# Two weight rings of unequal depth, the residual kept in DRAM, and gathers with an index bound, in a decoder layer with routed experts

## What is computed

```
x1     = x + gate1 * mixer(x)                       # the residual
h      = norm_modulate(x1)                          # rows of 1024 channels
scores = sigmoid(h @ w_router)                      # 64 experts in 8 groups
idx    = top 6 of the experts in the best 4 groups  # per token
routed = sum over the 6 of w * (silu(h @ w_gate[e]) * (h @ w_up[e])) @ w_down[e]
shared = (silu(h @ w_sg) * (h @ w_su)) @ w_sd
y      = norm_modulate(x1 + gate2 * (routed + shared))
```

## Time and profile before

| | us |
|---|---|
| three runs | 2287.98 (2282.24 to 2290.77), median and ends |
| profiled execution | 2288.57 |
| its span, first to last instruction | 2286.8 |
| TensorE busy | 1946.5 (85%) |
| VectorE / ScalarE / GpSimd busy | 869.4 / 470.1 / 217.9 |
| mean granted TensorE clock | 0.887 |

### The profile page before, as it was taken

One profiled execution on the slowest core, in us unless ns is written; L12 is line 12 of the kernel. 1 busy time (PEld: TensorE's weight loads), 2 busy tenths in 40 slices (PEclk: granted clock), 3 DMA queues, 4 the chain that ended last, 5 costly groups with the idle time before them and its releaser, 6 DMA issues.

```text
span 2286.8 us, 25257 instructions
## 1 busy us (share of the span) xinstructions
PE 1946.5 (85%) x8864; PEld 996.8 (44%) x8864; DVE 869.4 (38%) x2376; ACT 470.1 (21%) x899; POOL 217.9 (10%) x178
## 2 busy tenths in 40 slices
PE   3669899999988887979978989999999999895570
PEld 1146555554456663335555434444444443342230
DVE  4844711001255553222236234334433434331139
ACT  0121101210045551130143111111111111110022
POOL 0000001000000000030000011222122212111010
PEclk7679757899999999989987999999999999997785
DMA  8921002000102002521006179999999998896554
GB/s 293 358 54 51 3 0 116 1 0 1 74 13 71 1 1 92 186 102 55 0 39 155 47 291 313 350 358 348 342 354 346 368 376 280 282 330 221 202 166 179
DMA packets 98489, 389.72 MB, mean 170 GB/s; under 512 B 26879, under 2 KB 29603, under 8 KB 68780
## 3 DMA queue, kind: packets, MB, share of 16 engines
q1 hardware_dynamic: 79356, 318.89, 37.4%
q0 software_dynamic: 19008, 69.21, 11.6%
HBM read 329.43 MB, written 57.07 MB: 169 GB/s over the span
## 4 chain that ended last, share of the span: by engine, by line
PE 41%; DMA 6%; issue 5%; DVE 3%; ACT 2%; SPq 0%; POOL 0%; POOLq 0%; DVEq 0%; ACTq 0%
PE psum L1000 20%; PE psum L1011 9%; DMA arena<-in_w_exp_up 6%; PE psum L856 5%; PE psum L981 3%; PE psum L890 1%; PE psum L880 1%; PE psum L897 1%; PE psum L1018 1%; DVE arena L1686 1%; DVE arena L1675 0%; DVE arena L1687 0%; DVE arena L1676 0%; PE psum L835 0%; DVE arena L1674 0%
## 5 line engine op out<-in xcount | busy, mean ns | idle before, releaser
L1000 PE MATMUL psum<-arena 128*32 128x512 f32 (+2 forms) x2016 | 483.1, 614 | 86.1 <-DMA arena<-in_w_exp_up 84.8
L1000 PEld LDWEIGHTS psum<-arena 128*32 128x32 f32 (+2 forms) x2016 | 175.9, 143 | 340.1 <-issue 330.2
L1011 PE MATMUL psum<-arena,tail 128*32 128x512 f32 (+2 forms) x1000 | 231.6, 595 | 0.0
L1625 DVE TENSOR_TENSOR arena<-arena,psum 128x256 f32<-128x256 f32 x65 | 39.5, 608 | 445.2 <-ACT arena L1945 442.1
L2069 POOL DMA_INDIRECT moe_rows<-arena x64 | 101.6, 1588 | 682.6 <-DVE arena L1653 377.3
L1945 ACT ACTIVATE arena<-psum 128x256 f32<-128x256 f32 x65 | 24.9, 383 | 550.2 <-PE psum L1000 550.2
L704 PE MATMUL psum<-arena 128*128 128x512 f32 (+1 forms) x384 | 127.2, 495 | 0.0
L1011 PEld LDWEIGHTS psum<-arena,tail 128*32 128x32 f32 (+2 forms) x1000 | 79.9, 138 | 105.3 <-issue 105.3
L856 PE MATMUL psum<-arena 128*128 128x512 f32 (+1 forms) x288 | 124.3, 593 | 0.9 <-ACT arena L1871 0.5
L745 PE MATMUL psum<-arena 128*128 128x512 f32 (+2 forms) x192 | 85.0, 558 | 10.4 <-ACT arena L1801 10.4
L856 PEld LDWEIGHTS psum<-arena 128*128 128x128 f32 (+1 forms) x288 | 68.5, 239 | 55.3 <-issue 40.1
(11 more groups left out here) (478 smaller groups left out, 2436.6 us busy)
## 6 DMA issues: line engine op xcount, KB each, us to landing
arena<-in_w_exp_gate SPq DMA_DIRECT2D x66, 1024.0 KB, 13.6
arena<-in_w_exp_up SPq DMA_DIRECT2D x66, 1024.0 KB, 15.9
arena<-in_w_exp_down SPq DMA_DIRECT2D x66, 1024.0 KB, 14.8
arena<-in_w_ada SPq DMA_DIRECT2D x12, 2048.0 KB, 8.5
arena<-in_w_ada_final SPq DMA_DIRECT2D x4, 2048.0 KB, 8.3
arena<-in_cache_k SPq DMA_DIRECT2D x32, 256.0 KB, 3.9
arena<-in_cache_v SPq DMA_DIRECT2D x32, 256.0 KB, 2.9
arena<-moe_rows SPq DMA_DIRECT2D x16, 512.0 KB, 10.2
```

The source lines that it names most:

```text
L1000: ins = pe.matmul(slot[2 + par][lo:hi, :].rearrange("p (u n) -> p u n", u=2), xTs[:, par, k, lo:hi], gu, start=(k == 0), stop=(k == KD - 1))
L1011: ins = pe.matmul(slot[1][lo:hi, n * 512:(n + 1) * 512], hTs[:, k, lo:hi], ring[:, at, 2, k * D + n * 512:k * D + (n + 1) * 512], start=(k ...
```

## The change

- **Two rings.** The ring is split: six slots for gate and up (`GU_RING`), five for down (`DOWN_RING`). A gate-and-up slot is loaded again when the gate-and-up matmuls of its expert's last round are done, a down slot when the down projection of that round is done. SP issues gate and up of expert k, then down of expert k-1. The slots for the overflow experts get their release counts from two small tables that VectorE writes.
- **Residual in DRAM.** Four of the five down slots lie where x1 was. SP stores x1 to `x1_tiles` (4.46 MB, two DMAs) right behind the row stores, and loads it back tile by tile in the last stage; VectorE waits for three loads a tile there. The one-hot buffer moves to free the fifth slot.
- **Order.** `sorted_rounds` no longer balances step by step; it spreads the experts with more rounds than experts, and those with fewer, evenly over the list, and puts the single experts with two whole rounds at its end.
- **Gathers with a bound.** `g_idx` is now `row_all` as an integer, so an empty slot points behind the last token, and the gather has `bounds_check=T - 1, oob_is_err=False`, by which a row beyond the bound is left out. The scatter is as it was.
- At the end the release of a last, unused round of weights waits for one down projection.

```diff
@@ -63,7 +63,8 @@
 MAXPAIR = (T * TOPK // P + E + 1) // 2
-RING = 4
+GU_RING = 6
+DOWN_RING = 5
 MAXBLK = 128
@@ -90,11 +91,14 @@
     length = lambda it: -(-sum(CAPS[r] for r in it) // 4)
-    order, rounds, ahead = [], [], 0
-    while items:
-        it = min(items, key=lambda it: (abs(ahead + length(it) - len(it) - 1), len(it) if len(order) % 2 else -len(it), CAPS[it[0]]))
-        items.remove(it)
-        ahead += length(it) - len(it)
+    last = [it for it in items if len(it) < length(it) and len(it) == 1]
+    rest = [it for it in items if it not in last]
+    spread = []
+    for sign, shift in ((1, 0.2), (-1, 0.7), (0, 0.5)):
+        same = [it for it in rest if (length(it) > len(it)) - (length(it) < len(it)) == sign]
+        spread += [((i + shift) / len(same), it) for i, it in enumerate(same)]
+    order, rounds = [], []
+    for it in [it for _, it in sorted(spread)] + last:
         a, cap_a = len(order), CAPS[it[0]]
@@ -113,7 +117,7 @@
-assert NR % 2 == 0 and LAST_ROUND[E - RING] <= NR - 2
+assert NR % 2 == 0
@@ -167,6 +171,7 @@
         h2_dram = nc.dram_tensor("h2_rows", (T, D), F32, kind="Internal").ap()
+        x1_dram = nc.dram_tensor("x1_tiles", (P, NT * D), F32, kind="Internal").ap()
         y_dram = nc.dram_tensor("moe_rows", (2 * (T + P), D), F32, kind="Internal").ap()
@@ -329,7 +334,8 @@
         sh_d = arena(17152, 2, D)
-        ring = arena(4096, RING, 3, KD * FE)
+        gu_ring = arena(4096, GU_RING, 2, KD * FE)
+        down_ring = [arena(28672, 2 * D)] + [arena(39200 + 2 * D * i, 2 * D) for i in range(DOWN_RING - 1)]
         x_rows = arena(0, 2, D)
@@ -364,7 +370,7 @@
         tok_cols = arena(38736, 2, NT, 10, dt=BF16)
-        onehot = arena(28672, 2, NT, P, dt=BF16)
+        onehot = arena(34336, 2, NT, P, dt=BF16)
         xb = x_buf.rearrange("p a b -> p (a b)")
@@ -378,6 +384,9 @@
         row_off = arena(35780, 4)
+        release_f = arena(35784, 2 * MAXPAIR, parts=1)
+        release_gu = arena(35900, 2 * MAXPAIR, parts=1).bitcast(I32)
+        release_down = arena(38880, 2 * MAXPAIR, parts=1).bitcast(I32)
         row_all = arena(36064, NR + MAXBLK)
@@ -479,8 +488,8 @@
             "rank_step slot_step row_step pool_tick scattered routed_done rows_ready x2_ready x2_sq y_out_ready pad_scores cols_ready").split())
-        ld_gu = [sem(f"ld_gu{i}") for i in range(RING)]
-        ld_down = [sem(f"ld_down{i}") for i in range(RING)]
+        ld_gu = [sem(f"ld_gu{i}") for i in range(GU_RING)]
+        ld_down = [sem(f"ld_down{i}") for i in range(DOWN_RING)]
         gathered, stored_h2, stored_ys = ([sem(f"{n}{i}") for i in range(2)] for n in "gathered stored_h2 stored_ys".split())
@@ -981,14 +990,16 @@
-            def weights_of(b, par, pair, s_, n):
+            def weights_of(b, par, pair, loaded, n):
+                depth = len(loaded)
                 if isinstance(b, int) and b < NR:
                     for k in sorted({g[2] for g in ROUNDS[b]}):
-                        pe.wait_ge(s_[k % RING], n * (k // RING + 1))
-                    return [(lo * LANE, hi * LANE, RING - 1 - k % RING) for lo, hi, k in col_tiles(b)]
-                pe.wait_ge(s_[par], pair * n + n * (E // RING + 1))
-                return [(0, P, RING - 1 - par)]
+                        pe.wait_ge(loaded[k % depth], n * (k // depth + 1))
+                    return [(lo * LANE, hi * LANE, k % depth) for lo, hi, k in col_tiles(b)]
+                at = (E + par) % depth
+                pe.wait_ge(loaded[at], pair * n + n * (len(range(at, E, depth)) + 1))
+                return [(0, P, at)]
@@ -996,7 +1007,7 @@
                     for lo, hi, at in tiles:
-                        gu = ring[:, at, 0:2, k * FE:(k + 1) * FE]
+                        gu = gu_ring[:, GU_RING - 1 - at, :, k * FE:(k + 1) * FE]
                         ins = pe.matmul(slot[2 + par][lo:hi, :].rearrange("p (u n) -> p u n", u=2), xTs[:, par, k, lo:hi], gu, start=(k == 0), stop=(k == KD - 1))
@@ -1008,7 +1019,7 @@
                         for lo, hi, at in tiles:
-                            ins = pe.matmul(slot[1][lo:hi, n * 512:(n + 1) * 512], hTs[:, k, lo:hi], ring[:, at, 2, k * D + n * 512:k * D + (n + 1) * 512], start=(k == 0), stop=(k == 1))
+                            ins = pe.matmul(slot[1][lo:hi, n * 512:(n + 1) * 512], hTs[:, k, lo:hi], down_ring[at][:, k * D + n * 512:k * D + (n + 1) * 512], start=(k == 0), stop=(k == 1))
                 ins.then_inc(down_done, 1)
@@ -1532,6 +1543,12 @@
+            dlink(ts(release_f, iota_row[0:1, 0:2 * MAXPAIR], float(NR + 1), None, ALU.add))
+            for row, depth in ((release_gu, GU_RING), (release_down, DOWN_RING)):
+                for q in range(2):
+                    ins = dve.memset(release_f[:, q:q + 1], float(LAST_ROUND[E - depth + q] + 3))
+                dlink(ins)
+                dlink(cp(row, release_f))
             dlink(stt(cnt, cap_row, -float(LANE), cnt, ALU.mult, ALU.add))
@@ -1610,11 +1627,11 @@
                 rlink(tt(slot_v[:, 1:2], slot_v[:, 1:2], slot_v[:, 0:1], ALU.subtract), slot_step, i0 + 3)
-                cp(g_idx[:, par:par + 1], slot_v[:, 1:2])
                 rlink(ts(slot_v[:, 0:1], slot_v[:, 0:1], -1.0, 1.0, ALU.mult, ALU.add), slot_step, i0 + 4)
...
                 rlink(tt(slot_v[:, 2:3], slot_cols[:, par, 2:3], slot_cols[:, par, 3:4], ALU.add), slot_step, i0 + 5)
+                ts(g_idx[:, par:par + 1], row_all[:, at], 0.0, None, ALU.add)
                 tt(w_all[:, at], slot_v[:, 2:3], slot_cols[:, par, 4:5], ALU.add).then_inc(idx_done, 1)
@@ -1670,7 +1687,7 @@
                     m, s_ = rows(t), int(t == 8)
-                    dve.wait_ge(ld_y[t], 32)
+                    dve.wait_ge(ld_y[t], 48)
                     dlink(tt(y_rows[0:m, t, :], y_rows[0:m, t, :], y_rows2[t][0:m, :], ALU.add))
@@ -2054,7 +2071,8 @@
                 pool.sem_inc(pool_tick, 1)
-                pool.indirect_dma_start(x_rows[:, par, :], None, h2_dram, bass.IndirectOffsetOnAxis(ap=g_idx[:, par:par + 1], axis=0)).then_inc(gathered[par], 16)
+                pool.indirect_dma_start(x_rows[:, par, :], None, h2_dram, bass.IndirectOffsetOnAxis(ap=g_idx[:, par:par + 1], axis=0),
+                                        bounds_check=T - 1, oob_is_err=False).then_inc(gathered[par], 16)
@@ -2220,6 +2238,8 @@
             sp.sem_inc(rows_stored, 1)
+            dma(x1_dram[:, 0:8 * D], x1[:, 0:8, :].rearrange("p t d -> p (t d)")).then_inc(stored_h2[0], 16)
+            dma(x1_dram[0:NS, 8 * D:], x1[0:NS, 8, :]).then_inc(stored_h2[0], 16)
             sp.wait_ge(routed, 1)
@@ -2229,43 +2249,63 @@
-            def load_expert(e, q):
-                dst = ring[:, RING - 1 - q]
-                for i, w_e in enumerate((eg, eu, ed)):
-                    dma(dst[:, i, :], w_e[bass.ds(e, 1)].rearrange("a p n -> (a p) n")).then_inc(ld_gu[q] if i < 2 else ld_down[q], 16)
-            def load_sorted(k):
+            def load_gu(e, q):
+                for i, w_e in enumerate((eg, eu)):
+                    dma(gu_ring[:, GU_RING - 1 - q, i, :], w_e[bass.ds(e, 1)].rearrange("a p n -> (a p) n")).then_inc(ld_gu[q], 16)
+            def load_down(e, q):
+                dma(down_ring[q], ed[bass.ds(e, 1)].rearrange("a p n -> (a p) n")).then_inc(ld_down[q], 16)
+            def gu_sorted(k):
                 e = sp.value_load(sorted_i[0:1, ORDER[k]:ORDER[k] + 1], min_val=0, max_val=E - 1)
-                if k >= RING:
-                    sp.wait_ge(down_done, 2 + LAST_ROUND[k - RING] + 1)
-                load_expert(e, k % RING)
+                if k >= GU_RING:
+                    sp.wait_ge(gu_done, 3 + LAST_ROUND[k - GU_RING])
+                load_gu(e, k % GU_RING)
+                return e
+            def down_sorted(k, e):
+                if k >= DOWN_RING:
+                    sp.wait_ge(down_done, 3 + LAST_ROUND[k - DOWN_RING])
+                load_down(e, k % DOWN_RING)
...
             slots.wait_full(sp, ("W", NT - 1, 1))
-            load_sorted(0)
+            e_before = gu_sorted(0)
+            e_now = gu_sorted(1)
+            down_sorted(0, e_before)
             t = NT - 1
...
             store(sp, y_dram[t * P:t * P + rows(t), :], y_buf[0:rows(t), t % 2, :], stored_ys[t % 2])
-            for k in range(1, RING):
-                load_sorted(k)
+            sp.wait_ge(xn2_ready, NT)
+            sp.wait_ge(stored_h2[0], 112)
+            for k in range(2, GU_RING):
+                e_before, e_now = e_now, gu_sorted(k)
+                down_sorted(k - 1, e_before)
             sp.wait_ge(stored_ys[0], 80)
...
             sp.sem_inc(shared_stored, 1)
-            for k in range(RING, E):
-                load_sorted(k)
+            for k in range(GU_RING, E):
+                e_before, e_now = e_now, gu_sorted(k)
+                down_sorted(k - 1, e_before)
+            down_sorted(E - 1, e_now)
             sp.wait_ge(table_ready, 4)
...
                     e = sp.value_load(expert_i[0:1, bass.ds(j * 2 + q, 1)], min_val=0, max_val=E - 1)
```

(12 more changed lines are left out.)

## The result

The changed kernel took **2197.61 us** (median of 4 runs, 2193.46 to 2204.56) against 2285.11 for the kernel before (four runs beside it, 2282.14 to 2290.77), a ratio of 0.9617 [0.9584, 0.9651]. The prediction was 2200, in a range of 2182 to 2232. The profiled execution is the longest of the four, 2204.56 us: everything ahead of the shared expert, which the change does not touch, ended 10.4 us later in it (the row stores had landed at 1237.49 in place of 1227.13). So stages are compared by their own lengths, not by their place in the span.

What follows compares the result with a forecast made beforehand. TensorE, busy 85% of the span, was taken as the bound, with 102 us of waits for weights issued late. From 2288.6: -102 for waits, +12 and +1 for the residual, +0.3 for the release, so 2200 us, range 2182 to 2232.

Steps and rivals of the forecast that it cites:

- The 102 us of waits: TensorE's waits for weights with slow restarts, behind round 44 of the 64 rounds; all 102 us forecast to go.
- Nothing late in their place: 64 rounds: an expert loads in 10.9 us against one needed per 11.4, so no new weight waits.
- The reason lies in order and ring: Routed rounds: weights come late through expert order and four whole-expert slots freed only by a down projection; 102 us.
- The tight place at round 17: Early rounds: some 12 more experts needed by round 17, 11.8 us each against 10.9 to load one.
- Rounds of 766 us: 64 undisturbed rounds at 11.97 us each, taken from rounds 0 to 44 of the kernel before.
- The residual's way out, +12: Shared expert: store ahead of the zero fill delays a row store 11.3 us; TensorE stops 9, restart 3; ends 0 and 22.
- The way back and the release at the end, +1.3: Last stage: nine more residual loads, +1 us (+3 at 348 GB/s); SP waking for one more down projection, 0.3 us.
- cushion: Gathers skipping 8.9 MB, 0.33 us a round of transfers: 0 on the path, but spare supply for weights.
- the rival by which rounds 17, 36 and 55 would wait without it: Bound skips nothing in transfer time, so a few us of waits at those rounds: 2206 us, chance 0.04.
- Transfers: Rival in the rounds: transfers become the bound, some 25 us more, 2225 us; chance 0.19.
- hold-up at the start: Rival denied one: the residual's store fits beside the zero fill, -12 us, 2188 us; chance 0.11.
- The checked gather: Rival: GpSimd's index tests make each gather late, costing 64 times the excess over 2 us slack; chance 0.06.

Runs made afterwards that it cites:

- the late store: Changed kernel with the residual's store issued behind the shared expert's fourth row store in place of ahead of the zero fill: 2189.95 us, 0.9554 of the kernel before.
- the second profile of the same kernel: Changed kernel run again unaltered, as yardstick for follow-up runs: 2197.3 us, 0.9582 of the kernel before.

## Why the prediction was right, and where its reasons were not

**The 102 us of waits.** Right in size: the rounds lost 105.2 us and no wait for weights is left. "Nothing late in their place" held, and so did the rate it rested on: 377 GB/s over 40 us of rounds, near the 379 taken from the backlogged row.

The Trainium skill, page "HBM Reference", section "Specifications (TRN2)", has some 358 GB/s as the share of a core when both cores of a pair stream, and some 425 for a core that streams alone. This kernel ran on one core, and the trace agrees with the second: 421 in the store, and 377 over 40 us of mixed rounds, both above 358. So the prediction took the page's figure for a case that it does not describe, and the 5 to 10 us of waits worked out from it did not appear.

**Their cause.** Here the step failed that read "The reason lies in order and ring", and that priced order, depth and release as one. Taken apart one after the other, in us of the 64 rounds:

| what is added | rounds | difference |
|---|---|---|
| kernel before | 867.7 | |
| loads split, down of k - 1 behind gate and up of k (split, released late) | 856.1 | -11.6 |
| gate-and-up slots released by their own matmuls (split alone) | 776.6 | -79.5 |
| depth 6 and 5 (old order, everything else new) | 763.6 | -13.0 |
| new order (the whole change) | 762.5 | -1.1 |

Each is one profiled execution; the kernel before with the bound made 862.8, so differences of a few us here are not to be told apart. The row of the depth also has the bound in it, which the run without it shows to be worth nothing (762.0). The early release is three quarters of it in this sequence. The prediction named the late release as a cause ("a slot is freed only by a down projection") and the earlier one in a clause ("freed one matmul group earlier than now"), but gave it no price; its 16.5 us, a period of 11.97 and what lies behind the next gate and up, could have been read off the timeline of before. The order, half of the prediction's argument, is nothing beside the deep rings and +48.4 us without new ones. What a step is worth depends on what stands there already: the two more gate-and-up slots made 7.6 us with the new order (770.1 to 762.5). Six and five slots with the late release were not run, so it is shown that the early release does nearly all of it without the depth, and not that depth alone would not have done it. That the split's own 11.6 us (8.6 by the medians) come from the new sequence of loads is argued, not shown.

**The tight place at round 17** was real: with four gate-and-up slots round 17 waits 5.05 us, with six it does not.

**Rounds of 766 us** were 762.5, 11.91 a round in place of 11.97. The 526.45 us from which the 11.97 was taken hold three small waits for weights, 0.22, 1.47 and 0.18 us at rounds 19, 25 and 29. Without them it is 524.58 / 44 = 11.92 us, and 64 of these are 763.0; the prediction had these waits in the low end of its range only. (Of rounds 0 to 44 of the old order 18 are shared, not 19, which changes nothing here.) The longest of the three, in the kernel before:

```profile
1632.87 7.11 PE L1000 MATMUL psum<-arena 128*128 128x512 f32 x16 [1.47 <-DMA arena<-in_w_exp_up]
```

**The residual's way out, +12.** The mechanism held at each link, and the size was 9.6 (start 114.2 and the 0.9 us of the stores' issue, against 105.5). Two terms were mis-sized. The copy of tile 2, which the queue holds up, came 40.9 us behind the landing of the row stores in place of 1258.03 - 1227.13 = 30.9, so 10.0 us later and not 11.3: the store moved 421 GB/s where 394 were taken, which is 10.6 us for its 4.46 MB. So TensorE stopped for 7.4 us and not 9. And the restart cost 2.6 us in the two groups behind the stop (0.31 and 2.24), not 3. Against the changed kernel beside it the late store was worth 7.4 us, by the start alone 8.8 (114.0 and 0.9 against 106.1).

**The way back and the release at the end, +1.3.** The end grew by 1.2 us. SP's first load there was issued at 2134.71, 19.62 us after the last gate and up (19.60 before), so no run shows the 0.3 us of the release. The first addition came at 2141.92, 7.2 us later, where it had been 6.25; it waited for a load. In the second profile of the same kernel, whose end is as long, it came 6.0 us behind the first load, and the third tile waited 0.96 us instead. So the loads that came in addition cost the 1 us, at the first tile or at a later one. The first addition of the first profile, and the third of the second:

```profile
2141.92 1.22 DVE L1691 TENSOR_TENSOR arena<-arena 128x1024 f32<-128x1024 f32 x1 [10.89 <-DMA arena<-moe_rows]
...
2138.33 1.22 DVE L1691 TENSOR_TENSOR arena<-arena 128x1024 f32<-128x1024 f32 x1 [0.96 <-DMA arena<-moe_rows]
```

**The bound.** 8.9 MB less, no price on GpSimd that shows (1.04 us an instruction for 0.99), and 0 on the path, as forecast. But the "cushion" was not needed either: the rival by which rounds 17, 36 and 55 would wait without it, 2206, is shown wrong by the run without the bound.

**The other rivals.** Transfers were not the bound: with 8.9 MB more the rounds took 762.0 us. There was a hold-up at the start. The checked gather landed in 12.2 us in the median, sooner than the 13.2 of before.

**The sum.** 2288.6 - 105.2 + 9.6 + 1.2 = 2194.2: both terms that were off, by 3.2 and 2.4 us, had made the forecast too long. The profiled execution of 2204.6 is this and its late front part of 10.4; the second profile of the same kernel, with the fill issued at 1227.5 as before, took 2193.4. The median of 2197.6 lies between. So by the stages the forecast was 5.7 us too high, and that it came within 2.4 us of the median is in part luck: the front part, which the change does not touch, differs by over 10 us between the profiles.

## What to carry to other kernels

Before a ring is made deeper, ask by which of a slot's readers it is released: here a split and one earlier counter gave all but some 4 us of what a whole memory rearrangement gave, at the same bytes. A new order of demands is judged with the supply it will have; the same list was worth 1 us with one ring and cost 48 with another. What was put into the queue here was paid by the next thing in it that somebody waited for (10 us for one store, 11.6 more for a second), so a bulk store belongs behind the last small one that is urgent: moving it by a few lines took the price away.

## What the hardware showed beside

- Leaving rows out by the bound did not change the packet count: 19008 with and without it, while 8.9 MB went. The software queue's share fell from 11.9% of 2197.1 us to 11.0% of 2202.8 in the two changed kernels, 261 to 242 us of the 16 engines' time.
- The time from issue to landing rose while the waits went: the median for the three weight loads went from 13.6, 15.9 and 14.8 us to 17.0, 24.3 and 20.9, which fits loads issued earlier into a queue with more in it, though no run separates that. It is no measure of lateness.
- The zero fill moved 211 GB/s at 98% of the engines' time, a plain store from SBUF 421 at the same share. The fill reads one tile of 64 partitions again and again, the store reads 128 partitions; which of the two differences halves the rate no run here shows.
